# Light halves added on VectorE ahead of 64-row transposes; the heavy activations' low part by a product with minus identity and a copy on ScalarE

## The reference, cut to what matters

```python
def swiglu(h, wg, wu, wd):
    return (jax.nn.silu(h @ wg) * (h @ wu)) @ wd

def moe_swiglu(h, router, eg, eu, ed):
    b, s, d = h.shape
    t = h.reshape(b * s, d)
    logits = (t @ router).astype(jnp.float32)
    top_v, top_i = lax.top_k(logits, TOP_K)
    top_w = jax.nn.softmax(top_v, axis=-1)
    combine = jnp.sum(jax.nn.one_hot(top_i, N_EXPERTS, dtype=jnp.float32) * top_w[..., None], axis=1)
    out = jnp.zeros((b * s, d), jnp.float32)
    for e in range(N_EXPERTS):
        out = out + combine[:, e:e + 1] * swiglu(t, eg[e], eu[e], ed[e]).astype(jnp.float32)
    return out.astype(h.dtype).reshape(b, s, d)
```

## Time and profile before

| what | value |
|---|---|
| time, median of 3 runs | 1348.58 us (1347.03 to 1348.58) |
| the profiled execution | 1349.01 us, of which the span from first to last instruction is 1347.2 us |
| PE busy | 1316.7 us (98%), 6684 instructions |
| DVE busy | 1120.5 us (83%) |
| ACT busy | 941.3 us (70%) |
| chain that ended last | PE 86%, DVE 8%, ACT 2%, DMA 1% |
| HBM read | 430.04 MB |

### The profile page before, as it was taken

The page is one execution under the profiler, slowest core; times in us unless marked ns, Lnnn a source line. Parts: engine busy times, 40 slices in busy tenths (PEclk is TensorE's granted clock), DMA queues, the critical chain, the costliest instruction groups (busy, mean ns, idle before and its releaser), DMA issues.

```text
span 1347.2 us, 17501 instructions
## 1 busy us (share of the span) xinstructions
PE 1316.7 (98%) x6684; PEld 1094.6 (81%) x6685; DVE 1120.5 (83%) x1037; ACT 941.3 (70%) x879; POOL 103.0 (8%) x67
## 2 busy tenths in 40 slices
PE   8999999999999999999999999999999999999995
PEld 6898888887898778888888888888888888888873
DVE  5767655556766999999999999999999999999987
ACT  4645444444654777788787887888878788888875
POOL 1140000000231100100001000000000001000020
PEclk9999999999999999999999999999999999999998
DMA  9434655553423799999999999999999999999993
GB/s 354 186 104 165 226 189 188 190 188 129 186 96 141 291 365 382 406 408 419 411 400 420 417 413 404 415 418 395 416 420 405 418 405 408 416 421 415 408 421 132
DMA packets 63029, 437.47 MB, mean 325 GB/s; under 512 B 7231, under 2 KB 7409, under 8 KB 11746
## 3 DMA queue, kind: packets, MB, share of 16 engines
q1 hardware_dynamic: 58896, 423.23, 78.6%
q0 software_dynamic: 3904, 13.06, 2.6%
q10 hardware_dynamic: 146, 0.07, 0.0%
HBM read 430.04 MB, written 6.29 MB: 324 GB/s over the span
## 4 chain that ended last, share of the span: by engine, by line
PE 86%; DVE 8%; ACT 2%; DMA 1%; issue 1%; DVEq 0%; SPq 0%; ACTq 0%
PE ps L2117 34%; PE ps L2141 19%; PE ps L2237 8%; DVE w_lo L405 4%; PE ps L1805 4%; PE ps L2257 4%; PE ps L1820 4%; PE ps L1908 3%; PE ps L2246 2%; PE ps L1782 2%; PE ps L2133 1%; ACT w_hi L400 1%; DMA raw<-in_stream 1%; DVE spare_w L405 1%; PE ps L2177 1%
## 5 line engine op out<-in xcount | busy, mean ns | idle before, releaser
L405 DVE TENSOR_TENSOR w_lo<-raw,w_hi 128x2048 fp32r<-128x2048 f32 x313 | 715.3, 2303 | 125.2 <-ACT w_hi L400 124.2
L400 ACT ACTIVATE w_hi<-raw 128x2048 fp32r<-128x2048 f32 x315 | 599.8, 1917 | 162.1 <-PE ps L2117 66.2
L2117 PE MATMUL ps<-w_hi,xT_hi 128*128 128x512 f32 x564 | 224.0, 397 | 0.5 <-DVE xT_lo L1406 0.5
L2117 PE MATMUL ps<-w_lo,xT_hi 128*128 128x512 f32 x564 | 220.1, 390 | 0.0
L2117 PE MATMUL ps<-w_hi,xT_lo 128*128 128x512 f32 x564 | 219.5, 389 | 0.0
L405 DVE TENSOR_TENSOR spare_w<-raw,spare_w 128x2048 fp32r<-128x2048 f32 x85 | 194.5, 2288 | 9.8 <-ACT spare_w L400 9.6
L400 ACT ACTIVATE spare_w<-raw 128x2048 fp32r<-128x2048 f32 x85 | 163.0, 1918 | 18.5 <-PE ps L2141 16.0
L2117 PEld LDWEIGHTS ps<-w_lo,xT_hi 128*128 128x128 f32 x564 | 105.9, 188 | 22.8
L2117 PEld LDWEIGHTS ps<-w_hi,xT_hi 128*128 128x128 f32 x564 | 106.0, 188 | 21.5 <-DVE xT_lo L1406 0.7
L2117 PEld LDWEIGHTS ps<-w_hi,xT_lo 128*128 128x128 f32 x564 | 106.1, 188 | 20.8
L2141 PE MATMUL ps<-w_hi,aT_hi 128*128 128x512 f32 x288 | 114.0, 396 | 2.6 <-DVE w_lo L405 2.1
(11 more groups left out here) (352 smaller groups left out, 1979.6 us busy)
## 6 DMA issues: line engine op xcount, KB each, us to landing
raw<-in_stream SPq DMA_DIRECT2D x400, 1024.0 KB, 7.7
outs<-work POOLq DMA_DIRECT2D x5, 512.0 KB, 8.1
gain<-in_gains POOLq DMA_DIRECT2D x4, 512.0 KB, 5.5
h<-in_x SPq DMA_DIRECT2D x2, 512.0 KB, 6.7
raw<-in_stream SPq DMA_DIRECT2D x2, 512.0 KB, 6.3
tokens<-big POOLq DMA_DIRECT2D x2, 512.0 KB, 3.8
outs<-work POOLq DMA_DIRECT2D x4, 256.0 KB, 6.8
out<-work SPq DMA_DIRECT2D x4, 256.0 KB, 2.9
```

Of the source, the lines that this page charges most:

```text
L400: nc.scalar.activation(home(n, 0), raw[:, n % RAW, :], ACT.Copy).then_inc(hi_done, 1)
L405: nc.vector.tensor_tensor(home(n, 1), raw[:, n % RAW, :], home(n, 0).bitcast(F32), ALU.subtract).then_inc(lo_done, 1)
L2117: last = nc.tensor.matmul(ps[:, 4 + s, :], (xT_hi, xT_lo)[xp][:, k, x * P:(x + 1) * P], w((n + half), wp, kk * 512, (kk + 1) * 512), start ...
```

## The change

`fold` goes, and with it its matrix. In its place ScalarE copies only the lower half of each bank (64 rows, `low_copy`), VectorE adds the upper half of the bank to it (`pair_add`, two instructions in each step whose next pair is light), and PE transposes the 64-row sum (`turn_pair`, eight transposes). What waited for the copy (PE's turn, and `gate_up_free` of a light pair) now waits for the addition.

For a heavy pair VectorE's two subtractions go. ScalarE copies both blocks' high part in one instruction (`heavy_aT`); PE multiplies that high part with minus identity into the same banks, which leaves the low part there (`take_high`, two products of 256 columns, after block 0 of gate and up); ScalarE copies it out (`heavy_aT_lo`). Minus identity is written on VectorE in step 0, over the router's weights. The token numbers of `token_ids` become a product in fp32r of two columns.

```diff
@@ ACT @@
-            def pair_copy(par, n):
+            def low_copy(par, n):
                 used(act, n)
-                copy(g_sb[:, par, :], ps[:, 4 + par, :]).then_inc(pair_copied, 1)
+                copy(g_sb[0:LIGHT_ROWS, par, :], ps[LIGHT_ROWS:P, 4 + par, :]).then_inc(low_copied, 1)
+            def heavy_aT(B):
+                act.wait_ge(fm.aT_ps, B + 2)
+                copy(aT_hi[:, :, :, :].rearrange("p b f q -> p b (f q)"), ps[:, 6:8, 0:FB]).then_inc(fm.aT_hi, 2)
+            def heavy_aT_lo(i):
+                act.wait_ge(high_taken, 2 * i + 2 - FOLDED[i])
+                copy(aT_lo[:, :, :, :].rearrange("p b f q -> p b (f q)"), ps[:, 6:8, 0:FB]).then_inc(fm.aT_lo, 2)
...
                 else:
-                    ffn_aT(fm, 1, B, 0)
-                    ffn_aT(fm, 1, B + 1, 1)
+                    heavy_aT(B)
                 hi_unit(act, m + 4)
...
                     ffn_block(fm, 1, B + 2, 0, m + 2)
+                if not is_light:
+                    heavy_aT_lo(i)
                 hi_unit(act, m + 5)
@@ DVE @@
+            def pair_add(par, copied):
+                dve.wait_ge(low_copied, copied)
+                rows = g_sb[0:LIGHT_ROWS, par, :]
+                nc.vector.tensor_tensor(rows, ps[0:LIGHT_ROWS, 4 + par, :], rows, ALU.add).then_inc(pair_added, 1)
...
-                else:
-                    ffn_aT(fm, 1, B, 0)
-                    ffn_aT(fm, 1, B + 1, 1)
                 lo_unit(dve, m + 4)
                 if is_light:
                     light_lo(B, 0, 2)
-                if not next_light:
+                if next_light:
+                    pair_add(0, FOLDED[i + 1] + 1)
+                else:
                     ffn_block(fm, 1, B + 2, 0, m + 2)
                 if i == 0:
+                    nc.vector.tensor_copy(token_r[:, :, :], token.unsqueeze(2).to_broadcast([P, TT, 2]))
+                    nc.vector.tensor_scalar(minus_r, ident, -1.0, 0.0, ALU.mult, ALU.add).then_inc(minus_done, 1)
                     ranks()
...
                 lo_unit(dve, m + 6)
-                if not next_light:
+                if next_light:
+                    pair_add(1, FOLDED[i + 1] + 2)
+                else:
                     ffn_block(fm, 1, B + 3, 1, m + 4)
@@ PE @@
-            def fold(copied, par):
-                pe.wait_ge(pair_copied, copied)
+            def turn_pair(added, par):
+                pe.wait_ge(pair_added, added)
                 for c in range(4):
-                    last = nc.tensor.matmul(ps[:, 6 + par, c * LIGHT_ROWS:(c + 1) * LIGHT_ROWS], g_sb[:, par, c * P:(c + 1) * P],
-                                            fold_sum, start=True, stop=True, skip_group_check=True)
+                    last = nc.tensor.transpose(ps[:, 6 + par, c * LIGHT_ROWS:(c + 1) * LIGHT_ROWS],
+                                               g_sb[0:LIGHT_ROWS, par, c * P:(c + 1) * P], ident[0:LIGHT_ROWS, 0:LIGHT_ROWS])
                 last.then_inc(fm.aT_ps, 1)
+            def take_high(B):
+                if B == 0:
+                    pe.wait_ge(minus_done, 1)
+                pe.wait_ge(fm.aT_hi, B + 2)
+                for par in range(2):
+                    nc.tensor.matmul(ps[:, 6 + par, 0:FB], minus_r, aT_hi[:, par, :, :].rearrange("p f q -> p (f q)"), start=False,
+                                     stop=True, skip_group_check=True).then_inc(high_taken, 1)
...
                 else:
-                    pe.wait_ge(pair_copied, FOLDED[i] + par + 1)
+                    pe.wait_ge(pair_added, FOLDED[i] + par + 1)
...
                     whole(gu)
+                    if p < HEAVY:
+                        take_high(B)
                     bank_5_read(i - 1)
```

More of the change, by code:

```diff
@@ L234, in build @@
         w_slot = sb("w_slot", [P, 1])
+        token_r = sb("token_r", [P, TT, 2], F32R)
         ident = cst[:, C_ID:C_ID + P]
@@ L859, in step @@
                 if next_light:
[L860 removed]
+                    low_copy(1, m + 4)
                 else:
@@ L2240, in light_gate_up, with heavy_T @@
                     last.then_inc(unit_used, 1)
-            def fold(copied, par):
-                pe.wait_ge(pair_copied, copied)
+            def turn_pair(added, par):
+                pe.wait_ge(pair_added, added)
                 for c in range(4):
-                    last = nc.tensor.matmul(ps[:, 6 + par, c * LIGHT_ROWS:(c + 1) * LIGHT_ROWS], g_sb[:, par, c * P:(c + 1) * P],
-                                            fold_sum, start=True, stop=True, skip_group_check=True)
+                    last = nc.tensor.transpose(ps[:, 6 + par, c * LIGHT_ROWS:(c + 1) * LIGHT_ROWS],
+                                               g_sb[0:LIGHT_ROWS, par, c * P:(c + 1) * P], ident[0:LIGHT_ROWS, 0:LIGHT_ROWS])
                 last.then_inc(fm.aT_ps, 1)
+            def heavy_T(B, par):
+                pe.wait_ge(fm.mul, B + 1)
+                for f in range(2):
+                    last = nc.tensor.matmul(ps[:, 6 + par, f * P:(f + 1) * P], act_x[:, par, f * P:(f + 1) * P], ident, start=(f == 0),
+                                            stop=False, is_transpose=True, skip_group_check=True)
+                last.then_inc(fm.aT_ps, 1)
+            def take_high(B):
[5 more added lines that the diff above has]
+                                     stop=True, skip_group_check=True).then_inc(high_taken, 1)
             def light_down(B, par, n, first, final):
@@ L2277, in token_ids @@
                 for t in range(TT):
-                    last = nc.tensor.matmul(ps[:, 5, 0:1], disp[:, t, :].bitcast(F32), token[:, t:t + 1], start=(t == 0),
+                    last = nc.tensor.matmul(ps[:, 5, 0:2], disp[:, t, :], token_r[:, t, :], start=(t == 0),
                                             stop=(t == TT - 1), skip_group_check=True)
@@ L2381, in expert_step @@
                 if p < HEAVY:
-                    act_T(fm, 1, B, 0)
-                    act_T(fm, 1, B + 1, 1)
-                else:
-                    fold(FOLDED[i] + 1, 0)
-                    fold(FOLDED[i] + 2, 1)
+                    heavy_T(B, 0)
+                    heavy_T(B + 1, 1)
+                else:
+                    turn_pair(FOLDED[i] + 1, 0)
+                    turn_pair(FOLDED[i] + 2, 1)
                 bank_4_read(i - 1)
@@ L2420, in expert_step @@
                     if i == STEPS - 2:
-                        fold(FOLDED[i] + 3, 0)
+                        turn_pair(FOLDED[i] + 3, 0)
                     light_down(B + 1, 1, m + 5, False, final)
                     if i == STEPS - 2:
-                        fold(FOLDED[i] + 4, 1)
+                        turn_pair(FOLDED[i] + 4, 1)
             def over_expert(e, col, d):
```

11 lines of the change are left out of this document (5 added, 6 removed).

## The result

The changed kernel takes 1358.80 us (median of 5 runs, 1356.29 to 1361.85) beside 1348.58 (5 runs, 1347.03 to 1350.38). The ratio is 1.0072 with an interval of [1.0061, 1.0083]: slower by 0.7%, about 10 us. The forecast was no change, at 1350.1, with a range of its own from 1346 to 1352.5; over all its cases it reached from 1344 to 1355, so the result lies above all of it.

A forecast was written before the change was run, and what follows sets the result against it. PE was taken to set the pace, with DMA having little more to give. Start +3.8, middle -3.5 and end +1.2 summed to +1.5 us: 1350.5 for the execution, 1350.1 as median, range 1346 to 1352.5.

The forecast's parts named there:

- The prices: New work: light pair's turn 0.64 us on PE, two minus-identity products 0.23, VectorE's addition 0.6 from start to start.
- Step 0's gap of 2.8 us: Wait 1: PE stands 2.85 us in step 0 until VectorE has written minus identity; net +2.4 us.
- The five token steps: Steps 4, 15, 21, 36 and 41: gaps of 1.4 to 2.8 us on PE ahead of the token numbers.
- VectorE's total in the middle: 70 subtractions go (-23 us), 42 additions come (+25 us); VectorE's total stays.
- ScalarE's 20 us more: Larger copies for 35 heavy pairs add 19 us of ScalarE work, expected to cost no time.
- The ceiling of some 14 us in the middle: 560 to 1290 us: DMA at 420 GB/s instead of 412 lets the middle give back about 14 us at most.
- Wait 2: Token numbers before a light pair wait for VectorE's second addition: 1.4 us each, four in the middle +5.6 (0 to 11).
- The middle, -3.5: 560 to 1290 us: folds -17.4, heavy pairs +6.9, wait 2 +5.6 make PE -4.9; taken as -3.5 (-9 to +3).
- DMA takes back the start: Rival, chance 0.25: additions rarely waited for; start +1, middle -8, end +0.6, so 1342.2 us.
- The start, +3.8: Up to the first light pairs: step 0's wait, heavy products and wait 2 in step 4 cost +3.8 (0 to 4.5).
- The end, +1.2: After the last landing: two additions of 0.6 us on VectorE's chain, +1.2 (0.6 to 1.4).
- Additions clock PE: Rival, chance 0.30: token numbers and turns wait for VectorE's additions; start +4.4, middle +0.5, end +1.4, so 1354.9 us.

The follow-up runs named there:

- the light part: Only the changed kernel's edits for light pairs, heavy pairs as before, with the token products also moved behind the second down: 1338.93 us, ratio 0.9929.
- The kernel with filler: Changed kernel with unused products on PE ahead of step 0's wait and the five token waits: 1354.09 us, ratio 1.0036.
- late token products: Changed kernel with the token-number products behind the second down of their step instead of between the two downs: 1343.47 us, ratio 0.9961.
- both edits: Changed kernel with minus identity written early, ahead of step 0, and the token products behind the second down: 1342.27 us, ratio 0.9953.

## Why the prediction was wrong

**What held.** The prices: the turn 0.64 us, two products with minus identity 0.24, the addition 0.60 from start to start. Step 0's gap of 2.8 us ended by VectorE (2.67 of idle). The five token steps by name. VectorE's total in the middle, and ScalarE's 20 us more: PE waits for no copy of a low part between 560 and 1290. In step 4 such a copy is on the chain (0.60 us at 542.32), but only by a hair: the high part behind it ends at 544.73, and VectorE was busy until 544.71. The ceiling of some 14 us in the middle: the light part takes 22.9 us off PE and gains 10 of time, at 419 GB/s, though VectorE may have a share in that.

**The clock behind the waits is the first failed step.** It had no term; it stood only among what would make the forecast wrong. The changed kernel's profile has four drops before 1290 at up to 1.7 us, 6.8 together. Three of them, some 5 us, stand behind the new waits. The one at 445 does not (VectorE's low part of unit 72 behind it is 1.3 us late). Filling all six waits left no drop behind any of them and gave back 4.7 us of time. The clock also goes with the spread of 5.6 us among the changed kernel's runs: the execution of 1361.85 us had a mean clock of 0.987, that of 1356.29 had 0.992.

**Wait 2 is the second, a size.** The forecast counted 1.4 us for each token wait, 5.6 for the four of the middle, and set the one of step 4 against that pair's saving. Measured are 1.95, 2.60, 1.96, 1.97 and 2.60, near the 2.8 that I had worked out for VectorE from the earlier trace rows and then discounted, because VectorE "is not behind". It is: in step 4 PE starts the first down at 545.22, and VectorE at 544.75 still owes two low parts and an addition, 4.50 + 0.60 us on the chain, which the down covers for 2.72. Four waits of the middle come to 9.1.

**The middle, -3.5.** By work alone PE gains 10.5 us between units 108 and 372 (16 turns, 29 heavy pairs). The kernel with filler, which has the waits and no drops, changes by +0.4 us there, the changed one by +2.2, and those with late token products by -8.3 and -8.4. The difference of 8.7 is the four waits, and the further 1.8 the drop at 1052. The rival "DMA takes back the start" gave -8 for the middle: this is what the change is worth there once nobody waits. I had taken 1.4 us of PE's saving away for buffers that "don't smooth everything", and something of that size was seen: 2.1 are missing to PE's 10.5 without waits, 1.8 with them (-10.5 and 9.1 make -1.4, measured +0.4). What took them was not separated.

**The start, +3.8.** With the waits filled it is +3.9 at unit 108. In the changed kernel it is +8.2, and the difference of 4.3 is the three drops at 445, 472 and 551 (at most 5.1). As said, the one at 445 is not the change's.

**The end, +1.2.** From unit 396 (1314 us) on the changed kernel loses 2.0 us, that with both edits 1.2, that with all filler 4.4. In these profiles VectorE waited for the last gather 2.55 us, not at all, and 4.72 us. So the two additions can account for the 1.2, as forecast, and the gathers for the rest; no run takes the additions of the end alone, and why the gathers land late in some executions is open. A lower clock in the tail (1304 and 1335 in the changed kernel, 1326 in the one before) does not show there: PE's one piece of the chain from 1320 on takes 1.68 us after and 1.67 before.

**Sum.** 1350.5 for the execution by the forecast, 3.5 for the four waits, 6.8 for the drops and 0.8 for the end make 1361.6 against 1359.93. The excess of 1.7 has its place: between units 372 and 396, which no term covers, the changed kernel regains 1.5. "Additions clock PE" named the mechanism and the place, and gave 1354.9, which is close to the 1354.09 us of the kernel whose waits are all filled. Its start and middle (+4.4, +0.5) fit that kernel's +3.9 and +0.4; its end (+1.4 against +4.4) does not, and what that kernel regains between units 372 and 396 (2.2) makes up for most of it, so that the totals agree is in part luck. What no rival had was the clock.

## What to carry to other kernels

A wait on an engine that has no gaps is priced at its length plus what the clock does behind it: 1.8 to 2.7 us of idle were followed by a drop in about half of the cases here, which cost up to 1.7 us more, and in some twice that. Where work moves to an engine that is just behind, look at what stands on the waiting engine behind an instruction that newly waits for it: moving seven groups of small products by one place turned +0.7% into -0.4%. And test the parts singly: here the light part with the small products moved is the best kernel (1338.93 us, ratio 0.9929), and the heavy part costs time: +0.6% alone, with the wait of step 0 still in it, and 3.3 us when it stands beside the light part with both moves made. The heavy part alone without that wait was not run.

## What the runs showed of the hardware

- The granted clock of TensorE fell to its lower level (1.2 GHz) for 3.4 us, at times 6.8, at idle stretches of 1.8 to 2.7 us in an otherwise full stream; not at each. In the changed kernel it did at three of six such waits, over the eight profiles with unfilled waits at 16 of 30. It fell between 0.7 us before the end of the idle stretch and 1.8 us after it, and the five falls of 6.8 us at such waits all began 0.4 to 0.7 us before the end. With all six waits filled by unneeded products the next drop came only in the tail (1298 us).
- The same code before step 0 had a drop at 445 in the profile of the changed kernel and none in that of the kernel with filler, so it is not set by the instructions there alone. In the changed kernel PE was busy for 6.58 of the 7 us from 438 to 445.
- Eight f32 transposes of 64 rows by 128 columns took 0.64 us, in the new turn (L2266) as in the gather of a light expert (L2295), which has the same form. They are 8 instructions; the fold's eight f32 products were 16 (L2246 x16, 1.73 us), and filler of 8 products 16 too (L2456 x16, 1.78 us). Eight instructions fewer, at 0.08 to 0.11 us each, would be 0.6 to 0.9 of the 1.09 us that a turn saves, an estimate from these rows.
- Loads reached 417 to 419 GB/s as a mean over 730 us in the four changed kernels whose token products stand behind the second down. The Trainium skill, page "DMA: Bandwidth & Descriptors", section "Where 436 GB/s comes from", has HBM bind at about 358 GB/s for transfers between HBM and SBUF. The means of 408 to 419 GB/s from 560 to 1290 in these kernels lie above that, so it does not hold here; its fabric figure of 435 was not reached.
